# Embedding stage of a two-layer hybrid block: the order of its loads and of VectorE's turns

## Chip, cores and metric

The kernel runs on one core of one Trainium2 chip. The metric is the device time of one execution in microseconds (us), lower is better. The engines are TensorE (PE), VectorE (DVE), ScalarE (ACT), GpSimd (POOL) and SyncE (SP, which here only issues transfers).

## What is computed

A row of 1024 tokens with 1024 features goes through a layer norm and then through two layers, each a projection into a state-space part, latent attention, retention and sparse attention, an output projection, and an MLP:

```python
h = layer_norm(x, ln_emb_g, ln_emb_b)
for l in range(2):
    parts = split_columns(h @ w_in[l])        # the first 260 columns: z (256) and dt (4)
    ...
    h = layer_norm(ALPHA * h + mix, ln1_g[l], ln1_b[l])
    ff = square(relu(h @ w_mlp1[l])) @ w_mlp2[l]
    h = layer_norm(ALPHA * h + ff, ln2_g[l], ln2_b[l])
# layer_norm: (x - mean) * rsqrt(var + 1e-5) * g + b
```

The change touches only the first line and the 260 columns of z and dt of layer 0, which are projected in the same stage.

## The kernel before

The stage `embed` holds the whole of `h` in SBUF as eight tiles of 128 tokens (one token per partition, 1024 features in a row). Products are made to nearly full float32 precision by splitting each operand into a high part (rounded to fp32r) and a low part (the rest), and taking three products: high x high, high x low, low x high. Each engine has its own instruction list; semaphores tie them together, and each engine runs its list in order.

What happens to tile t, and where it stands in the code:
- SP loads `h[:, t, :]` (L195). Behind tile 1 it issues the two loads of z and dt weights (`load_columns`, L338, into `ahead`, seen through `raw`) and the gain row and the bias row of the norm, each spread over all 128 partitions (L198, L199: 512 KB each, as large as a tile).
- VectorE, `moments(t)`: two `bn_stats` (L213), `bn_aggr` (L215), add of epsilon to the variance (L217).
- GpSimd, `rstd(t)`: the power -0.5 of one column (L263).
- VectorE, the shift, -mean x rstd, one column, both inputs in SBUF (L241).
- ScalarE centres the tile: x x rstd + shift (L290).
- VectorE, `finish(t)`: the tile times the gain row, the gain product (L222), both inputs in SBUF.
- GpSimd adds the bias row (L271), both inputs in SBUF. For tile 7 VectorE does it itself (L226). Then the tile is ready (`normed`): SP stores it to `residual` (L204), and TensorE turns it, eight transposes of 128x128 into two banks of PSUM (L323).
- ScalarE, `highs(t)`: two copies from PSUM, the high parts of the turned tile (L285). VectorE, `lows(t)`: two subtractions, PSUM minus high part, the low parts `x_lo` (L233).
- TensorE, `project(t)`: 24 products of the turned tile with the z weights (L363 to L365). ScalarE, `take(t)`: two copies out of PSUM (L278, L279), which also wait until the store of the tile is done, since they overwrite `h`.

Once per stage, the z weights are split: ScalarE copies each half (L295, after it has centred tile 0), VectorE subtracts each half (L246, in turn 0), both inputs in SBUF. Behind that (`w_lo`) SP issues the next weights' load (L203) and then the stores, and TensorE may start its first projection.

The order of VectorE's list is written out by hand: `moments(0)`, and then for each turn t: `moments(t + 1)`, shift(t), in turn 0 the split, `finish(t - 1)`, `lows(t - 3)`. TensorE's: transposes of t, `project(t - 2)`. GpSimd's: `rstd(0)`, `rstd(1)`, and then `rstd(t + 2)`, bias add of t. The stage ends with a barrier of all engines behind the last `take`; the next stage's work begins behind it.

Of the kernel before, what the change touches and what calls it, by code (L numbers as in the profile page):

```python
# [23 lines left out]
ALU = mybir.AluOpType  # L24
# [6 lines left out]
NT = T // P  # L31
# [137 lines left out]
def embed(nc, x, gain, bias, h, dtr, residual, hi, lo, ahead, ident, next_w):  # L169
# [5 lines left out]
    with ExitStack() as c:  # L175
        n = norm_tiles(nc, c, "emb")
# [10 lines left out]
        LAG = 2  # L187
        x_loaded = [s.x_loaded0, s.x_loaded1, s.x_loaded2, s.x_loaded3, s.x_loaded4, s.x_loaded5, s.x_loaded6, s.x_loaded7]
        with nc.Block() as block:
            first_loads = ahead.count + 16 * len(projection_groups()[0].parts)  # L190

            @block.sync
            def _(sp):
                for t in range(NT):
                    sp.dma_start(h[:, t, :], x[t * P:(t + 1) * P, :]).then_inc(x_loaded[t], 16)  # L195
                    if t == 1:
                        load_columns(sp, ahead, next_w, 0)
                        sp.dma_start(n.gain[:], gain.partition_broadcast(P)).then_inc(s.gains_loaded, 16)  # L198
                        sp.dma_start(n.bias[:], bias.partition_broadcast(P)).then_inc(s.gains_loaded, 16)  # L199
                sp.wait_ge(s.w_lo, 2)  # L200
                load_columns(sp, ahead, next_w, 1)
                for t in range(NT):
                    sp.wait_ge(s.normed, t + 1)  # L203
                    sp.dma_start(residual[t * P:(t + 1) * P, :], h[:, t, :]).then_inc(h_stored[t], 16)  # L204
                for t in range(NT):
                    sp.wait_ge(h_stored[t], 16)

            @block.vector
            def _(dve):
                def moments(t):  # L210
                    dve.wait_ge(x_loaded[t], 16)
                    for half in range(2):
                        dve.bn_stats(n.stats[:, t, half, :], h[:, t, half * 512:(half + 1) * 512]).then_inc(s.stats_ready, 1)  # L213
                    dve.wait_ge(s.stats_ready, 2 * t + 2)
                    dve.bn_aggr(n.mv[:, t, :], n.stats[:, t, :, :].rearrange("p a b -> p (a b)")).then_inc(s.moments_ready, 1)  # L215
                    dve.wait_ge(s.moments_ready, t + 1)
                    dve.tensor_scalar(n.var[:, t:t + 1], n.mv[:, t, 1:2], EPS, None, ALU.add).then_inc(s.var_ready, 1)  # L217

                def finish(t):
                    dve.wait_ge(s.centred, t + 1)  # L220
                    dve.wait_ge(s.gains_loaded, 32)
                    dve.tensor_tensor(h[:, t, :], h[:, t, :], n.gain[:], ALU.mult).then_inc(s.scaled, 1)  # L222
                    if t == NT - 1:
                        dve.wait_ge(s.scaled, NT)
                        dve.wait_ge(s.normed, NT - 1)
                        dve.tensor_tensor(h[:, t, :], h[:, t, :], n.bias[:], ALU.add).then_inc(s.normed, 1)  # L226

                def lows(t):
                    for half in range(2):
                        g = 2 * t + half  # L230
                        dve.wait_ge(s.hi_copied, g + 1)
                        part = slice(4 * half, 4 * half + 4)
                        dve.tensor_tensor(lo[:, part, t * P:(t + 1) * P], tr[:, g % 6, :].rearrange("p (k n) -> p k n", k=4),  # L233
                                          hi[:, part, t * P:(t + 1) * P].bitcast(F32), ALU.subtract).then_inc(s.lo_copied, 1)

                moments(0)
                for t in range(NT):
                    if t + 1 < NT:
                        moments(t + 1)
                    dve.wait_ge(s.rstd_ready, t + 1)  # L240
                    dve.scalar_tensor_tensor(n.shift[:, t:t + 1], n.mv[:, t, 0:1], -1.0, n.rstd[:, t:t + 1], ALU.mult,  # L241
                                             ALU.mult).then_inc(s.shift_ready, 1)
                    if t == 0:
                        for part in range(2):
                            dve.wait_ge(s.w_hi, part + 1)
                            dve.tensor_tensor(wlo[:, k_half(part), :], raw[:, k_half(part), :], whi[:, k_half(part), :].bitcast(F32),  # L246
                                              ALU.subtract).then_inc(s.w_lo, 1)
                    if t:
                        finish(t - 1)
                    if t >= 3:  # L250
                        lows(t - 3)
                finish(NT - 1)
                lows(NT - 3)
                lows(NT - 2)
                lows(NT - 1)

            @block.gpsimd
            def _(pool):
                pool.memset(n.power[:], -0.5).then_inc(s.power_set, 1)
                pool.wait_ge(s.power_set, 1)  # L260
                def rstd(t):
                    pool.wait_ge(s.var_ready, t + 1)
                    pool.tensor_tensor(n.rstd[:, t:t + 1], n.var[:, t:t + 1], n.power[:], ALU.pow).then_inc(s.rstd_ready, 1)  # L263

                rstd(0)
                rstd(1)
                for t in range(NT - 1):
                    if t + 2 < NT:
                        rstd(t + 2)
                    pool.wait_ge(s.scaled, t + 1)  # L270
                    pool.tensor_tensor(h[:, t, :], h[:, t, :], n.bias[:], ALU.add).then_inc(s.normed, 1)  # L271

            @block.scalar
            def _(act):
                def take(t):
                    act.wait_ge(s.z_ready, t + 1)
                    act.wait_ge(h_stored[t], 16)
                    act.activation(h[:, t, GW:2 * GW], zp[:, t % 2, 0:GW], ACT.Copy)  # L278
                    act.activation(dtr[:, t, :], zp[:, t % 2, GW:FIRST], ACT.Copy).then_inc(s.z_taken, 1)  # L279

                def highs(t):
                    for half in range(2):
                        g = 2 * t + half
                        act.wait_ge(s.turned, g + 1)
                        act.activation(hi[:, 4 * half:4 * half + 4, t * P:(t + 1) * P], tr[:, g % 6, :].rearrange("p (k n) -> p k n", k=4),  # L285
                                       ACT.Copy).then_inc(s.hi_copied, 1)

                for t in range(NT):
                    act.wait_ge(s.shift_ready, t + 1)
                    act.activation(h[:, t, :], h[:, t, :], ACT.Identity, bias=n.shift[:, t:t + 1],  # L290
                                   scale=n.rstd[:, t:t + 1]).then_inc(s.centred, 1)
                    if t == 0:
                        act.wait_ge(ahead.sem, first_loads)
                        for part in range(2):
                            act.activation(whi[:, k_half(part), :], raw[:, k_half(part), :], ACT.Copy).then_inc(s.w_hi, 1)  # L295
                    if t >= 3:
                        highs(t - 3)
                    if t >= 3 + LAG:
                        take(t - 3 - LAG)
                for t in range(NT - 3, NT):  # L300
                    highs(t)
                    take(t - LAG)
                for t in range(NT - LAG, NT):
                    take(t)

            @block.tensor
            def _(pe):
                def project(t):
                    pe.wait_ge(s.w_lo, 2)
                    pe.wait_ge(s.lo_copied, 2 * t + 2)  # L310
                    if t >= 2:
                        pe.wait_ge(s.z_taken, t - 1)
                    first_unit(pe, zp[:, t % 2, 0:FIRST], hi, lo, whi, wlo, t).then_inc(s.z_ready, 1)

                for t in range(NT):
                    pe.wait_ge(s.normed, t + 1)
                    for half in range(2):
                        g = 2 * t + half
                        if g >= 6:
                            pe.wait_ge(s.lo_copied, g - 5)  # L320
                        for j in range(4):
                            k = 4 * half + j
                            mm = pe.transpose(tr[:, g % 6, j * P:(j + 1) * P], h[:, t, k * P:(k + 1) * P], ident[:])  # L323
                        mm.then_inc(s.turned, 1)
                    if t >= LAG:
                        project(t - LAG)
                for t in range(NT - LAG, NT):
                    project(t)
# [2641 lines left out]
```

## Time and profile before

| | |
|---|---|
| median of 3 runs | 2829.88 us (2828.07 to 2831.41) |
| profiled execution, its own time | 2830.91 us |
| its span in the trace | 2829.1 us |
| mean granted clock of TensorE | 0.977 |
| PE busy | 2658.6 us, 94% |
| DVE busy | 1894.8 us, 67% |
| ACT busy | 1285.5 us, 45% |
| POOL busy | 309.5 us, 11% |
| tile 0 lands / last `take` starts | 7.0 us / 62.97 us |

Times in the trace count from the start of the span. The device time of the profiled execution is 1.8 us more than the span. A granted clock of 1.00 is TensorE at 2.4 GHz, 0.50 is 1.2 GHz. The embedding stage is the first 64 us.

### The profile page before, as it was taken

Reading aid. Unit: us, or ns where it says so; the run is one execution under the profiler, and the core shown is the slowest. Engines: PE = TensorE matmul, PEld = TensorE weight load, DVE = VectorE, ACT = ScalarE, POOL = GpSimd, SP = SyncE. Lnnn points to the kernel's source line nnn. Section 1 sums busy time; section 2 is a strip of 40 time slices with the busy share of each in tenths; the row PEclk is TensorE's granted clock in tenths of the full one; section 3 lists DMA queues with packets and bytes.
Section 4 is the critical chain, followed back from the end, with each engine's and each line's share of the span. In section 5 each row is a group of like instructions: output and inputs, shape, how many; then the busy total and the mean of one; then the engine's idle time right before and its main releaser. Section 6 shows DMA issues by size and latency. Waiting matters only on the chain. (4 is left out here: it accounts for less than half of the span.)

```text
span 2829.1 us, 39315 instructions
## 1 busy us (share of the span) xinstructions
PE 2658.6 (94%) x14644; PEld 2273.5 (80%) x14644; DVE 1894.8 (67%) x2993; ACT 1285.5 (45%) x2327; POOL 309.5 (11%) x304
## 2 busy tenths in 40 slices
PE   5999989888989999999999999898899899999997
PEld 5899868777868887888888998686778688878886
DVE  5654546576777776686856444566766877758778
ACT  3332236666355554433433222556643555543343
POOL 3121223111000000000011212221110000000000
PEclk9999999999999999999999999899999999999998
DMA  4223323102315445987621233330032354479865
GB/s 165 71 68 89 96 80 95 38 1 83 112 62 173 144 143 185 384 316 246 237 86 39 78 100 97 93 90 1 1 125 84 97 164 152 142 266 361 291 228 188
DMA packets 256563, 387.11 MB, mean 137 GB/s; under 512 B 40760, under 2 KB 129272, under 8 KB 256376
## 3 DMA queue, kind: packets, MB, share of 16 engines
q1 hardware_dynamic: 256376, 384.61, 42.1%
q8 instruction: 119, 1.95, 0.3%
q14 instruction: 68, 0.56, 0.1%
HBM read 287.73 MB, written 96.83 MB: 136 GB/s over the span
## 5 line engine op out<-in xcount | busy, mean ns | idle before, releaser
L2863 DVE TENSOR_TENSOR att_el<-att_ET,att_eh 128x512 fp32r<-128x512 f32 (+1 forms) x228 | 151.3, 671 | 97.5 <-ACT att_eh L2805 96.0
L636 POOL TENSOR_TENSOR norm_rstd<-norm_var,norm_power 128x1 f32<-128x1 f32 x32 | 28.9, 904 | 1471.9 <-DVE norm_var L616 1471.9
L1618 PE MATMUL mix_acc<-mix_whi,x_hi 128*128 128x256 f32 (+1 forms) x640 | 185.4, 290 | 0.0
L2805 ACT ACTIVATE att_eh<-att_ET 128x512 fp32r<-128x512 f32 (+1 forms) x228 | 131.6, 584 | 108.7 <-PE att_ET L2713 74.0
L990 PE MATMUL dense_tr<-mlp_w,mlp_a 128*128 128x512 f32 x448 | 175.3, 391 | 5.4 <-DVE mlp_w L1294 5.4
L1620 PE MATMUL mix_acc<-mix_whi,x_lo 128*128 128x256 f32 (+1 forms) x640 | 180.0, 281 | 0.0
L1619 PE MATMUL mix_acc<-mix_wlo,x_hi 128*128 128x256 f32 (+1 forms) x640 | 179.9, 281 | 0.0
L2796 ACT ACTIVATE att_E<-att_S,att_negm 128x64 f32<-128x64 f32 (+8 forms) x256 | 155.4, 616 | 45.6 <-DVE att_negm L2856 29.9
L990 PE MATMUL dense_acc<-mlp_w,mlp_a 128*128 128x512 f32 x448 | 174.8, 390 | 0.0
L992 PE MATMUL dense_tr<-mlp_w,mlp_a 128*128 128x512 f32 x448 | 174.8, 390 | 0.0
L991 PE MATMUL dense_acc<-mlp_w,mlp_a 128*128 128x512 f32 x448 | 174.6, 390 | 0.0
L991 PE MATMUL dense_tr<-mlp_w,mlp_a 128*128 128x512 f32 x448 | 174.6, 390 | 0.0
L992 PE MATMUL dense_acc<-mlp_w,mlp_a 128*128 128x512 f32 x448 | 174.5, 390 | 0.0
L2856 DVE TENSOR_REDUCE att_negm<-att_S 128x1 f32<-128x640 f32 (+12 forms) x160 | 136.6, 860 | 53.4 <-PE att_S L2692 50.0
L1098 ACT ACTIVATE mlp_a<-mlp_a_raw 128x1024 fp32r<-128x1024 f32 x72 | 76.3, 1060 | 166.9 <-PE dense_tr L992 137.7
L2713 PE MATMUL att_ET<-ident,att_E 128*128 128x128 f32 (+1 forms) x880 | 135.3, 279 | 14.0 <-DVE att_el L2863 13.9
L1292 DVE TENSOR_TENSOR mlp_a<-mlp_a_raw,mlp_a 128x1024 fp32r<-128x1024 f32 x72 | 88.0, 1222 | 65.7 <-ACT mlp_a L1098 65.7
L1619 PEld LDWEIGHTS mix_acc<-mix_wlo,x_hi 128*128 128x128 f32 x640 | 122.8, 192 | 0.1
L1618 PEld LDWEIGHTS mix_acc<-mix_whi,x_hi 128*128 128x128 f32 x640 | 122.7, 192 | 0.1
L1583 POOL TENSOR_TENSOR mix_wlo<-ahead,mix_whi 128x2048 fp32r<-128x2048 f32 (+2 forms) x22 | 94.3, 4288 | 258.9 <-ACT mix_whi L1800 258.9
L1620 PEld LDWEIGHTS mix_acc<-mix_whi,x_lo 128*128 128x128 f32 x640 | 122.6, 192 | 0.0
L1233 DVE TENSOR_TENSOR h<-h 128x512 f32<-128x512 f32 x160 | 99.1, 685 | 34.7 <-issue 30.6
(431 smaller groups left out, 7815.4 us busy)
## 6 DMA issues: line engine op xcount, KB each, us to landing
mlp_w_raw<-w_mlp SPq DMA_DIRECT2D x124, 512.0 KB, 6.1
blocks<-h SPq DMA_DIRECT2D x32, 1792.0 KB, 8.8
mlp_a_raw<-blocks SPq DMA_DIRECT2D x72, 512.0 KB, 4.5
mlp_raw<-w_mlp SPq DMA_DIRECT2D x66, 512.0 KB, 6.0
ahead<-w_in SPq DMA_DIRECT2D x20, 1024.0 KB, 6.9
mlp_temp<-blocks SPq DMA_DIRECT2D x38, 512.0 KB, 5.0
residual<-h SPq DMA_DIRECT2D x32, 512.0 KB, 3.2
h<-residual SPq DMA_DIRECT2D x32, 512.0 KB, 6.9
```

What stands on the lines that cost most here:

```text
L990: pe.matmul(out, ah, wh, start=(ch == 0 and k == 0), stop=False, skip_group_check=True)
L991: pe.matmul(out, ah, wl, start=False, stop=False, skip_group_check=True)
L992: mm = pe.matmul(out, al, wh, start=False, stop=(ch == CH - 1 and k == 1), skip_group_check=True)
L1233: mm = dve.tensor_tensor(stage[g % 2][:, i - 1, :], part[a], part[b], op)
L1618: pe.matmul(out, xh, whi[b][:, k, 0:n], start=(k == 0), stop=False)
L1619: pe.matmul(out, xh, wlo[b][:, k, 0:n], start=False, stop=False)
L1620: mm = pe.matmul(out, xl, whi[b][:, k, 0:n], start=False, stop=(k == KT - 1))
L2713: mm = pe.transpose(ET[0:kw, o % 2, j * P:(j + 1) * P], E[:, p.unit % KEPT, at:at + kw], ident[:])
L2796: e = act.activation(E[:, n % KEPT, here], S[:, n % 2, here], ACT.Exp, bias=negm[:, n, r:r + 1], accum_out=den[:, d, h:h + 1])
L2805: act.activation(eh[0:kw, k % RING, cols], ET[0:kw, nth[x] % 2, cols], ACT.Copy).then_inc(s.high_ready, 1)
L2856: dve.tensor_reduce(negm[:, n, first:len(q.rows):step], view[:, first:len(q.rows):step, 0:width], AX.X, ALU.max, negate=True).then_inc(s.m ...
L2863: dve.tensor_tensor(el[0:kw, k % RING, cols], ET[0:kw, nth[x] % 2, cols], eh[0:kw, k % RING, cols].bitcast(F32), ALU.subtract).then_inc(s. ...
```

## The change

The gain and bias rows are issued behind tile 0, the two z loads behind tile 2. In VectorE's list the shift of tile t stands ahead of `moments(t + 1)`; the gain product of tile t comes in turn t instead of turn t + 1; the split of the z weights stands in turn 2 behind that product; `lows(t - 2)` takes the place of `lows(t - 3)`. GpSimd does the bias add of t ahead of `rstd(t + 2)`. ScalarE casts the z weights in turn 2, and its `highs` and `take` come one turn sooner. TensorE's list stays.

```diff
--- before.py
+++ after.py
@@ -193,10 +193,11 @@
             def _(sp):
                 for t in range(NT):
                     sp.dma_start(h[:, t, :], x[t * P:(t + 1) * P, :]).then_inc(x_loaded[t], 16)
-                    if t == 1:
-                        load_columns(sp, ahead, next_w, 0)
+                    if t == 0:
                         sp.dma_start(n.gain[:], gain.partition_broadcast(P)).then_inc(s.gains_loaded, 16)
                         sp.dma_start(n.bias[:], bias.partition_broadcast(P)).then_inc(s.gains_loaded, 16)
+                    if t == 2:
+                        load_columns(sp, ahead, next_w, 0)
                 sp.wait_ge(s.w_lo, 2)
                 load_columns(sp, ahead, next_w, 1)
                 for t in range(NT):
@@ -235,22 +236,19 @@
 
                 moments(0)
                 for t in range(NT):
-                    if t + 1 < NT:
-                        moments(t + 1)
                     dve.wait_ge(s.rstd_ready, t + 1)
                     dve.scalar_tensor_tensor(n.shift[:, t:t + 1], n.mv[:, t, 0:1], -1.0, n.rstd[:, t:t + 1], ALU.mult,
                                              ALU.mult).then_inc(s.shift_ready, 1)
-                    if t == 0:
+                    if t + 1 < NT:
+                        moments(t + 1)
+                    finish(t)
+                    if t == 2:
                         for part in range(2):
                             dve.wait_ge(s.w_hi, part + 1)
                             dve.tensor_tensor(wlo[:, k_half(part), :], raw[:, k_half(part), :], whi[:, k_half(part), :].bitcast(F32),
                                               ALU.subtract).then_inc(s.w_lo, 1)
-                    if t:
-                        finish(t - 1)
-                    if t >= 3:
-                        lows(t - 3)
-                finish(NT - 1)
-                lows(NT - 3)
+                    if t >= 2:
+                        lows(t - 2)
                 lows(NT - 2)
                 lows(NT - 1)
 
@@ -265,10 +263,10 @@
                 rstd(0)
                 rstd(1)
                 for t in range(NT - 1):
+                    pool.wait_ge(s.scaled, t + 1)
+                    pool.tensor_tensor(h[:, t, :], h[:, t, :], n.bias[:], ALU.add).then_inc(s.normed, 1)
                     if t + 2 < NT:
                         rstd(t + 2)
-                    pool.wait_ge(s.scaled, t + 1)
-                    pool.tensor_tensor(h[:, t, :], h[:, t, :], n.bias[:], ALU.add).then_inc(s.normed, 1)
 
             @block.scalar
             def _(act):
@@ -289,15 +287,15 @@
                     act.wait_ge(s.shift_ready, t + 1)
                     act.activation(h[:, t, :], h[:, t, :], ACT.Identity, bias=n.shift[:, t:t + 1],
                                    scale=n.rstd[:, t:t + 1]).then_inc(s.centred, 1)
-                    if t == 0:
+                    if t == 2:
                         act.wait_ge(ahead.sem, first_loads)
                         for part in range(2):
                             act.activation(whi[:, k_half(part), :], raw[:, k_half(part), :], ACT.Copy).then_inc(s.w_hi, 1)
-                    if t >= 3:
-                        highs(t - 3)
-                    if t >= 3 + LAG:
-                        take(t - 3 - LAG)
-                for t in range(NT - 3, NT):
+                    if t >= 2:
+                        highs(t - 2)
+                    if t >= 2 + LAG:
+                        take(t - 2 - LAG)
+                for t in range(NT - 2, NT):
                     highs(t)
                     take(t - LAG)
                 for t in range(NT - LAG, NT):
```

## Rows read from the trace of the kernel before

**Rows 1.** Timeline of ScalarE, embedding
```profile
12.27 2.03 ACT L295 ACTIVATE emb_whi<-ahead 128x1040 fp32r<-128x1040 f32 x2 [0.54 <-DMA ahead<-w_in]
...
23.60 1.24 ACT L290 ACTIVATE h<-h,emb_shift,emb_rstd 128x1024 f32<-128x1024 f32 x1 [2.62 <-DVE emb_shift L241]
...
57.23 0.38 ACT L278 ACTIVATE h<-emb_zp 128x256 f32<-128x256 f32 x1 [2.24 <-PE emb_zp L365]
...
62.97 0.39 ACT L278 ACTIVATE h<-emb_zp 128x256 f32<-128x256 f32 x1 [2.42 <-PE emb_zp L365]
```

**Rows 2.** Timeline of VectorE, embedding: start us, us, what, count [idle before <-releaser]
```profile
13.37 2.40 DVE L246 TENSOR_TENSOR emb_wlo<-ahead,emb_whi 128x1040 fp32r<-128x1040 f32 x2 [2.92 <-ACT emb_whi L295]
...
19.61 1.22 DVE L222 TENSOR_TENSOR h<-h,emb_gain 128x1024 f32<-128x1024 f32 x1
...
22.37 1.19 DVE L241 SCALAR_TENSOR_TENSOR emb_shift<-emb_mv,emb_rstd 128x1 f32<-128x1 f32 x1
...
29.22 1.29 DVE L233 TENSOR_TENSOR x_lo<-emb_tr,x_hi 128x512 fp32r<-128x512 f32 x2 [0.66 <-ACT x_hi L285]
...
32.12 1.22 DVE L222 TENSOR_TENSOR h<-h,emb_gain 128x1024 f32<-128x1024 f32 x1
...
36.89 1.22 DVE L222 TENSOR_TENSOR h<-h,emb_gain 128x1024 f32<-128x1024 f32 x1
...
50.40 1.22 DVE L226 TENSOR_TENSOR h<-h,emb_bias 128x1024 f32<-128x1024 f32 x1
```

**Rows 3.** Timeline of VectorE and GpSimd in the last layer norm
```profile
2807.38 1.29 DVE L609 BATCH_NORM_STATS2 norm_stats<-h 128x6 f32<-128x512 f32 x2
...
2809.03 1.23 DVE L627 TENSOR_TENSOR h<-h,norm_gain 128x1024 f32<-128x1024 f32 x1
...
2809.18 1.48 POOL L636 TENSOR_TENSOR norm_rstd<-norm_var,norm_power 128x1 f32<-128x1 f32 x1 [2.67 <-DVE norm_var L616]
...
2810.70 0.16 DVE L621 SCALAR_TENSOR_TENSOR norm_shift<-norm_mv,norm_rstd 128x1 f32<-128x1 f32 x1 [0.44 <-POOL norm_rstd L636]
```

**Rows 4.** Timeline of GpSimd, embedding
```profile
19.71 1.53 POOL L263 TENSOR_TENSOR emb_rstd<-emb_var,emb_power 128x1 f32<-128x1 f32 x1 [8.68 <-DVE emb_var L217]
21.21 2.33 POOL L271 TENSOR_TENSOR h<-h,emb_bias 128x1024 f32<-128x1024 f32 x1
```

**Rows 5.** Timeline of SP's queue, embedding
```profile
3.42 0.81 SPq L195 DMA_DIRECT2D h<-x  x2
...
8.91 0.43 SPq L199 DMA_DIRECT2D emb_bias<-ln_emb_b  x1
```

**Rows 6.** Landing times of tiles 0 and 1 (L195), then of the bias row (L199)
```profile
DMA to landing us min/median/max: 3.6/4.1/4.5
...
DMA to landing us min/median/max: 7.7/7.7/7.7
```

**Rows 7.** Timeline of GpSimd and VectorE in attention, 1944.9 to 1945.2 us
```profile
1944.93 0.73 POOL L2600 TENSOR_TENSOR h<-h,att_total 128x256 f32<-128x256 f32 x1
1944.96 0.72 DVE L2878 TENSOR_TENSOR att_factor<-att_factor,att_gates 128x4 f32<-128x4 f32 x1
```

**Rows 8.** Timeline of GpSimd and VectorE in the dense part, about 1351 us
```profile
1350.77 1.52 POOL L636 TENSOR_TENSOR norm_rstd<-norm_var,norm_power 128x1 f32<-128x1 f32 x1 [11.10 <-DVE norm_var L616]
...
1351.80 1.22 DVE L1294 TENSOR_TENSOR mlp_w<-mlp_raw,mlp_w 128x1024 fp32r<-128x1024 f32 x1
```

**Rows 9.** Timeline of TensorE: the last eight transposes of the embedding
```profile
53.27 1.03 PE L323 MATMUL emb_tr<-ident,h 128*128 128x128 f32 x8
```

**Rows 10.** Windows: stretch, us, busy (count) by engine, granted clock, DMA share, GB/s
```profile
66.00:70.00 4.00, 4.00 (x12) 3.11 (x11) 1.44 (x3) 0.48 (x1) 0.00 (x0) 0.57 0.49 4
...
383.90:387.30 3.40, 2.10 (x6) 1.25 (x7) 0.00 (x0) 0.00 (x0) 0.00 (x0) 1.00 0.67 216
...
524.00:527.20 3.20, 1.46 (x7) 0.66 (x6) 0.69 (x1) 1.66 (x4) 0.00 (x0) 1.00 0.00 0
527.20:530.60 3.40, 1.12 (x4) 0.72 (x4) 2.49 (x6) 1.29 (x3) 0.62 (x1) 0.50 0.00 0
```

## The prediction

> **What bounds the kernel now.** I read the page first: TensorE is busy for 94% of the span (the table above), so a stage in front of it hands its delay on almost whole. The change touches only the embedding stage, from 3.4 us to the barrier behind the last copy of the projected columns. So I read the timelines of the engines there, one by one, and asked what paces a tile. What ends the stage is TensorE: the copies that wait for a finished projection start at 57.23 and (two tiles later) at 62.97 us, 2.87 us apart, back to back [rows 1]. The reader is to see that TensorE gets there only because VectorE and GpSimd fed it early enough: gain products start some 3.9 us apart at first (19.61, and the second right behind the shift of 22.37) and 4.77 us apart from the fourth on (32.12, 36.89) [rows 2]. A late VectorE would therefore show at the end.
>
> Two facts about that pair of engines carry the argument. First, the shift (0.16 us where nothing is in its way [rows 3]) took 1.19 us at 22.37 and ended at 23.56; GpSimd's bias add ran from 21.21 for 2.33, to 23.54 [rows 2, 4]. A VectorE instruction whose two inputs are in SBUF stands still while GpSimd's add runs; the subtractions of x_lo, with one input in PSUM, took 1.29 for two at 29.22, beside the next add, and lost nothing [rows 2]. Second, the square root behind a gain product ends 0.41 us after the product: 2809.03 + 1.23 = 2810.26 and 2809.18 + 1.48 = 2810.66 [rows 3].
>
> **The change part by part.** *Loads.* SP issues the gain and bias rows behind tile 0. Before, tiles 0 and 1 land at 3.4 + 3.6 = 7.0 and 3.8 + 4.5 = 8.3 us, the bias row at 8.91 + 7.7 = 16.6 [rows 5, 6], and the cast that waits for the z loads starts at 12.27 [rows 1]. Tile 1 now comes behind two more transfers of its own size. Lower bound: each takes the 1.3 us between tiles 0 and 1, so it lands at 7.0 + 3 x 1.3 = 10.9. Upper bound: the two rows take what they took before, 16.6 - 12.3 = 4.3, so 8.3 + 4.3 = 12.6. The rows do not say which holds (whatever drew out the two rows may or may not return), so I take the middle, 11.8. Tile 2 follows 1.3 later and z behind it; both are there before they are asked for. The three SP instructions that change places cost nothing else.
>
> *The moments moved behind the shift.* This is what costs. Before, moments(t+1) ran while GpSimd added the bias of t-1, and then shift and gain product followed at once. Now the order is shift(t), moments(t+1), gain product(t), subtractions(t-2) from tile 2 on, shift(t+1). Counting from the start of gain product(t):
> - the product ends at 1.23; the square root of t+1, asked for just after the product began, ends at 1.23 + 0.41 = 1.64 [rows 3];
> - GpSimd goes straight on to the bias add of t. At 21.21 such an add began 0.03 before the square root ahead of it ended (19.71 + 1.53 = 21.24) [rows 4]; VectorE, waiting for the same square root, begins its shift 0.04 after it (2810.66 to 2810.70) [rows 3]. So the add leads by 0.06 to 0.07 us. In attention a lead of 0.03 us was enough: the add at 1944.93 ran 0.73, the product at 1944.96 took 0.72 for four elements [rows 7]. The shift waits for the whole add, until 1.61 + 2.33 + 0.02 = 3.96. From tile 2 on it comes behind the two subtractions, in the middle of the add, and waits with no doubt;
> - then the moments: from the first statistics to the gain product 2809.03 - 2807.38 = 1.65, and a VectorE instruction behind the shift starts some 0.08 before it ends (2810.70 + 0.16 against 2810.77) [rows 3]. Next product: 3.96 - 0.08 + 1.65 = 5.53.
>
> ScalarE's centring (1.24) [rows 1] lies beside the moments. The subtractions (1.29) lie beside the add. So a turn takes 5.53 us where it took 3.9 or 4.77. The moments were hidden by the add, and the new order takes that cover away; that the bias add comes before the next square root on GpSimd removes nothing, since the add must wait for the product anyway.
>
> *The split of z, two turns later.* In turn 2 ScalarE casts the halves behind its centring (2.03 for both) [rows 1] and VectorE subtracts them, 2.40 for both before [rows 2]. Both inputs are in SBUF. The first half starts right behind the gain product; the small square root that waits then does not delay it (1351.80 took 1.22 with one waiting since 1350.77) [rows 8]. It ends about 2.4 after the product's start. The bias add of tile 2 has waited and now runs to about 2.35 + 2.3 = 4.65; the second half waits for it and ends 1.1 later, 5.75; the subtractions of tile 0 end at 6.95; shift and moments follow (1.65), product 3 starts at about 8.6. A turn of 8.6 instead of 5.53: 3.05 more. Before, the split lay in the wait for tile 2 and cost nothing.
>
> The Trainium skill (SBUF — State Buffer, section Who interferes with whom) says that the SBUF port pair which VectorE and GpSimd share is an exclusive lock, held for the whole instruction. By that sentence the square root would also hold up the first half of the split by 0.4 us, and the sum would be 4.7 where it is 4.3; the row of the trace shows no such delay, and it decides.
>
> *Sum.* With tile 1 at L = 11.8, product 0 starts at L + 1.65 = 13.45. Products 1 and 2: +5.53 each, 24.5. Product 3: +8.6, 33.1. Products 4 to 6: 3 x 5.53, 49.7. Product 7 needs no moments before it, only the centring: 3.96 + 0.04 + 1.24 + 0.03 = 5.27, so 55.0. The bias add of tile 7 on VectorE ends 2.5 later (1.23 + 0.03 + 1.22 [rows 2]), 57.5; subtractions of tile 5, 1.2, end at 58.7. TensorE by then has turned tile 7 (1.0 [rows 9]) and has three projections left: 3 x 2.87 + 0.03 = 8.65 [rows 1]. Last copy at about 67.3 instead of 62.97: **+4.3 us**. With the bounds for L, 66.4 to 68.1: +3.4 to +5.1. TensorE's own work (1.0 + 2.9 a turn) fits in 5.53 and is no bound from tile 3 on. The stores of the rows queue behind the later w_lo wait on SP, and behind them ScalarE's copies wait, but these come a turn of 5 us later still; I cost that at nothing. If a store were late there, it would hold the centring behind the copy and cost what it is late.
>
> The profiled execution took 2830.91 for a span of 2829.1, 1.0 above the median of 2829.88. Its sum gives 2835.2; against the median I predict **2834.2 us**. A measurement of this kernel tells about 0.2% (5.7 us) from no change, so this is a loss inside that bound.
>
> **The rivals.**
> 1. *My forecast*, the shift held up in every turn: +3.4 to +5.1, chance 0.62. The stage's end also meets TensorE's clock: behind it came 4.0 us with a mean granted clock of 0.57 [rows 10], which is 3.4 us at 1.2 instead of 2.4 GHz and loses 1.7 of work. Whether that returns at the shifted time moves the result by up to that.
> 2. *The shift slips in ahead of the add* in turns 0 and 1, since only 0.06 us decide. Then the moments lie beside the add, the next product starts at its end, 3.95, and two turns save 1.58 each: +4.3 - 3.2 = +1.1, 2831.0. The row with a lead of 0.03 speaks against it. Chance 0.11.
> 3. *The clock falls inside the stage* (the one that ends slower by over 0.2%). TensorE is busy for 3.9 of 5.53 us from tile 3 on. In a stretch with 2.10 of 3.40 us busy it kept 1.00; behind one with 1.46 of 3.20 it ran at 0.50 [rows 10]. My share, 0.71, is above both, but it is made of idle gaps of 1.6 us. One such fall in the last turns costs about 1.7 (three projections that nothing hides), 2834.2 + 1.7 = 2835.9; two give 2837.6. It decides only if it falls from product 6 on; earlier the idle 1.6 us a turn take it up. Chance 0.19.
> 4. *VectorE is not held up as I think*, for instance because the 1.19 us of the old shift have another cause. Then a turn is VectorE's own 1.15 + 1.2 + 0.07 + 1.65 = 4.1, the early rows pay, and TensorE becomes the bound: first projection at about 28, eight projections of 2.87 and five turnings of 1.0 end at 56.0, and half of the first at the lower clock adds 1.4: 57.4, -5.5, 2824.4. Against it stand the matching ends of shift and add. Chance 0.08.
>
> **How the numbers follow.** The likeliest is rival 1's middle, 2834.2; its own range is 2833.3 to 2835.0 by L alone, 2831.6 to 2836.7 with the clock. The 8-in-10 range takes in rival 2 and most of rival 3: 2830.0 to 2837.5. Slower by over 0.2% (above 2835.5): rival 3 with 0.13 of its 0.19, and 0.13 from the upper end of rival 1: 0.26. Faster (below 2824.2): half of rival 4, 0.04. Within: 0.70.
>
> **What would show it.** In the profile after: gain products 5.5 us apart with a gap of 8.6 behind the third; all shifts but the first at over 2 us (turns 0 and 1) or some 1.5 (later), ending with a bias add; the second half of the split at over 2 us; tile 1's statistics at 10.9 to 12.6; the last copy of emb_zp at 66.4 to 68.1. Shifts of 0.15 in turns 1 and 2 mean rival 2, in all turns rival 4. A granted clock below 1.00 between 45 and 68 us means rival 3. Wrong outright would be a stage end before 63 us, or one past 70, which would mean a wait for a store or a load that I cost at nothing.

## The result, and the profile after

The changed kernel has a median of 2835.12 us (22 runs, 2829.66 to 2837.51) against 2829.30 us of 22 runs of the kernel before beside it: ratio 1.0019 [1.0013, 1.0025]. It is slower by 5.8 us, a loss that the measurement tells from zero. It lies on the edge of the prediction's bound of 0.2%: the ratio is just inside (0.19%), the two medians just outside (5.8 for 5.7 us). It is 0.9 above the predicted 2834.2, and inside its range. The last copy of emb_zp, which closes the embedding stage, starts at 68.11 us instead of 62.97: +5.14, just at the upper end of the +3.4 to +5.1 that the prediction gave. The profiled span is 2833.7 us with a mean granted clock of 0.978.

Busy times of the engines, from the page of the changed kernel:

```profile
PE 2658.4 (94%) x14644; PEld 2272.2 (80%) x14644; DVE 1903.8 (67%) x2993; ACT 1284.7 (45%) x2327; POOL 310.0 (11%) x304
```

TensorE does what it did. VectorE is "busy" for 9.0 us more with the same instructions, 8.9 of it in the embedding (39.3 us of the first 64 before, 48.2 of the first 69 now): a VectorE instruction that stands still behind GpSimd is counted as running, so the waits hide in durations and not in idle time. Timeline of VectorE in the embedding (start us, us, what, count, idle before it and its releaser), which answers to [rows 2]:

```profile
12.40 1.29 DVE L214 BATCH_NORM_STATS2 emb_stats<-h 128x6 f32<-128x512 f32 x2 [3.04 <-DMA h<-x]
...
14.05 1.23 DVE L223 TENSOR_TENSOR h<-h,emb_gain 128x1024 f32<-128x1024 f32 x1
15.73 2.29 DVE L240 SCALAR_TENSOR_TENSOR emb_shift<-emb_mv,emb_rstd 128x1 f32<-128x1 f32 x1 [0.45 <-POOL emb_rstd L261]
...
19.57 1.23 DVE L223 TENSOR_TENSOR h<-h,emb_gain 128x1024 f32<-128x1024 f32 x1
...
25.07 1.23 DVE L223 TENSOR_TENSOR h<-h,emb_gain 128x1024 f32<-128x1024 f32 x1
26.22 4.53 DVE L248 TENSOR_TENSOR emb_wlo<-ahead,emb_whi 128x1040 fp32r<-128x1040 f32 x2
...
33.57 1.22 DVE L223 TENSOR_TENSOR h<-h,emb_gain 128x1024 f32<-128x1024 f32 x1
34.71 1.28 DVE L234 TENSOR_TENSOR x_lo<-emb_tr,x_hi 128x512 fp32r<-128x512 f32 x2
35.91 1.63 DVE L240 SCALAR_TENSOR_TENSOR emb_shift<-emb_mv,emb_rstd 128x1 f32<-128x1 f32 x1
...
39.10 1.23 DVE L223 TENSOR_TENSOR h<-h,emb_gain 128x1024 f32<-128x1024 f32 x1
...
55.43 1.22 DVE L223 TENSOR_TENSOR h<-h,emb_gain 128x1024 f32<-128x1024 f32 x1 [1.31 <-ACT h L288]
56.69 1.23 DVE L227 TENSOR_TENSOR h<-h,emb_bias 128x1024 f32<-128x1024 f32 x1
```

Timeline of GpSimd in the same stretch, which answers to [rows 4]:

```profile
15.66 2.33 POOL L267 TENSOR_TENSOR h<-h,emb_bias 128x1024 f32<-128x1024 f32 x1
...
25.23 1.48 POOL L261 TENSOR_TENSOR emb_rstd<-emb_var,emb_power 128x1 f32<-128x1 f32 x1 [1.72 <-DVE emb_var L218]
26.68 2.97 POOL L267 TENSOR_TENSOR h<-h,emb_bias 128x1024 f32<-128x1024 f32 x1
...
35.17 2.35 POOL L267 TENSOR_TENSOR h<-h,emb_bias 128x1024 f32<-128x1024 f32 x1
```

Read the two side by side. The shift at 15.73 writes one column, and takes 2.29 us: it ends at 18.02, the add of 15.66 at 17.99. The add had a lead of 0.07 us. The shift at 35.91 comes in the middle of the add of 35.17 and ends at 37.54, the add at 37.52. Gain products start 5.52, 5.50, 8.50, and then 5.53 us apart; the last gap is 5.28.

Timeline of ScalarE, the last copies that wait for a projection, against those of [rows 1]; then the eight transposes of tile 7 on TensorE; then the window from 45 to 68 us (busy time and count of PE, PEld, DVE, ACT and POOL, granted clock, DMA share, GB/s):

```profile
65.24 0.38 ACT L276 ACTIVATE h<-emb_zp 128x256 f32<-128x256 f32 x1 [2.43 <-PE emb_zp L363]
...
68.11 0.38 ACT L276 ACTIVATE h<-emb_zp 128x256 f32<-128x256 f32 x1 [2.42 <-PE emb_zp L363]
```

```profile
57.99 1.08 PE L321 MATMUL emb_tr<-ident,h 128*128 128x128 f32 x8
```

```profile
45.00:68.00 23.00, 19.76 (x162) 18.99 (x160) 15.10 (x20) 9.15 (x23) 7.38 (x4) 1.00 0.18 74
```

Behind VectorE's last add (56.69 + 1.23 = 57.92) come one turning on TensorE, beside the subtractions of tile 5 on VectorE, and three projections, at the full clock.

### The profile page after: what moved, and what is told of

It is laid out like the page before. It is cut to its first block and busy times, and to the rows that moved or that the text cites. A ratio compares the mean times of both kernels' runs of the same rounds, so it can differ in the third digit from the quotient of the medians.

```text
span 2833.7 us, 39315 instructions
## 1 busy us (share of the span) xinstructions
PE 2658.4 (94%) x14644; PEld 2272.2 (80%) x14644; DVE 1903.8 (67%) x2993; ACT 1284.7 (45%) x2327; POOL 310.0 (11%) x304
```

## The experiments

Every kernel below has 10 or 11 runs, timed against 33 runs of the kernel before on the same chip (medians 2829.29 and 2829.24 on the two chips used); the change itself has 22 against 22. "Stage end" is the start of the last copy of emb_zp in one profiled execution. It is the cleaner measure, but not to the last tenths: in the five kernels with the rows behind tile 0 (the change among them), tile 1 landed between 11.87 and 12.40 us. Whole spans carry TensorE's clock in the other 2760 us with them (a span of 2819.9 with 0.981 and one of 2833.7 with 0.978 lie 13.8 apart, and their stage ends 8.5).

| kernel | stage end | median, us | ratio to before |
|---|---|---|---|
| before | 62.97 | 2829.3 | |
| the change | 68.11 | 2835.12 | 1.0019 [1.0013, 1.0025] |
| change, one-input shift | 59.65 | 2826.01 | 0.9989 [0.9980, 0.9998] |
| before, one-input shift | 62.22 | 2829.57 | 0.9998 [0.9990, 1.0007] |
| change, moments ahead | 68.91 | 2835.39 | 1.0022 [1.0013, 1.0031] |
| loads and split alone | 63.59 | 2830.09 | 1.0000 [0.9992, 1.0009] |
| order alone | 65.13 | 2831.47 | 1.0011 [1.0002, 1.0020] |
| change, rows behind tile 1 | 63.67 | 2830.52 | 1.0005 [0.9996, 1.0014] |
| change, low parts between halves | 66.54 | 2833.02 | 1.0014 [1.0005, 1.0023] |
| order alone, one-input shift | 56.63 | 2824.11 | 0.9982 [0.9973, 0.9991] |

### The shift with one input

The theory is that the shift is held because both its inputs are tiles in SBUF. So the same product is written with the rstd as the scalar operand and only the mean as input, in the changed kernel, where it should free the loop, and in the kernel before, where the add paces the loop anyway.

```diff
-dve.scalar_tensor_tensor(n.shift[:, t:t + 1], n.mv[:, t, 0:1], -1.0, n.rstd[:, t:t + 1], ALU.mult,
-                         ALU.mult).then_inc(s.shift_ready, 1)
+dve.tensor_scalar(n.shift[:, t:t + 1], n.mv[:, t, 0:1], n.rstd[:, t:t + 1], -1.0, ALU.mult,
+                  ALU.mult).then_inc(s.shift_ready, 1)
```

> The changed kernel, with the shift computed from one SBUF tensor and a per-partition scalar (tensor_scalar) in place of two SBUF tensors (scalar_tensor_tensor); same numbers. My theory: the shift no longer waits for GpSimd's bias add. Shifts take about 0.15 us in every turn, gain products come 4.0 to 4.1 us apart where the changed kernel has 5.53, TensorE becomes the bound behind tile 6 and the last copy of emb_zp starts at 60 to 61 us (68.1 in the changed kernel, 62.97 before): 7 to 8 us faster than the changed kernel, some 2 us faster than before. Rival A, the wait belongs to GpSimd's add whatever form the shift has: nothing moves, last copy at 68.1, shifts of 1.6 to 2.3 us. Rival B, the shift's wait is only a symptom and moments, centring or loads set the turn: shifts of 0.15 us but turns still above 5 us.

> The kernel before, with the same one-input shift. My theory: there the shift's wait was hidden, because the gain product behind it has to wait for the end of the same bias add. Last copy of emb_zp within 0.3 us of 62.97, ratio to before 1.000. The rival, that the wait had cost the kernel before as well, gives the last copy up to 2 us earlier (two waits of 1.0 us at 22.4 and 26.2 us).

Timeline of all engines in the changed kernel with this shift, 15.0 to 17.6 us:

```profile
15.23 2.34 POOL L267 TENSOR_TENSOR h<-h,emb_bias 128x1024 f32<-128x1024 f32 x1
15.29 0.21 DVE L240 TENSOR_SCALAR emb_shift<-emb_mv,emb_rstd 128x1 f32<-128x1 f32 x1 [0.45 <-POOL emb_rstd L261]
15.42 1.27 DVE L214 BATCH_NORM_STATS2 emb_stats<-h 128x6 f32<-128x512 f32 x2
...
17.05 1.60 DVE L223 TENSOR_TENSOR h<-h,emb_gain 128x1024 f32<-128x1024 f32 x1
```

Same place, same lead of the add (0.06 us), and the shift takes 0.21 us where it took 2.29. The moments now lie beside the add, and the product itself, which has two inputs, waits for its end (17.57) and takes 1.60. From tile 3 on the turn is 4.09 us, where it was 5.53. The stage ends 8.46 us sooner than with the change (0.43 of it tile 1, that landed sooner, at 11.97) and 3.32 sooner than before. So the hold on this one instruction is what the change pays for, and without it the rest of the change would have been a gain: 2826.01, 0.9989 [0.9980, 0.9998].

The Trainium skill (SBUF — State Buffer, section Who interferes with whom) says that a VectorE instruction with at most one SBUF input, outside the two-port modes, does not contend with GpSimd, and that one with two does where GpSimd reads SBUF. The trace agrees: 0.21 us against 2.29 beside the same add. The edit changes the instruction too, and not only its inputs; but the gain product, another instruction with two inputs in SBUF, is held in this kernel and the next (1.60 and 2.13), and the subtractions, with one input in PSUM, are not (1.29 in the next kernel, at 33.13, beside the add of 32.85).

In the kernel before, all engines from 21 to 24 us:

```profile
21.18 2.33 POOL L271 TENSOR_TENSOR h<-h,emb_bias 128x1024 f32<-128x1024 f32 x1
...
22.34 0.20 DVE L241 TENSOR_SCALAR emb_shift<-emb_mv,emb_rstd 128x1 f32<-128x1 f32 x1
22.46 2.13 DVE L222 TENSOR_TENSOR h<-h,emb_gain 128x1024 f32<-128x1024 f32 x1
```

The shift is free here too, and most of the wait moves into the product behind it: 22.46 + 2.13 = 24.59, where before the shift was 22.37 + 1.19 and the product then took 1.21, to 24.69. The stage ends at 62.22, 0.75 sooner, where 62.97 within 0.3 was expected: a small miss, since a shift that is held also holds up ScalarE. ScalarE's and VectorE's timelines in this kernel, tile 0:

```profile
27.52 1.06 ACT L285 ACTIVATE x_hi<-emb_tr 128x512 fp32r<-128x512 f32 x2
28.32 1.27 DVE L233 TENSOR_TENSOR x_lo<-emb_tr,x_hi 128x512 fp32r<-128x512 f32 x2
```

In ScalarE's list the centring of tile 3 stands ahead of these copies. In the kernel before, the shift of tile 3, held to 27.43, let the centring start at 27.47 and the copies at 28.61, and VectorE stood idle 0.66 us for them before the subtractions of 29.22 [rows 2]. Here the centring starts at 26.38, and the subtractions follow the product at once, 0.90 sooner. The fourth gain product starts at 31.25 instead of 32.12, and VectorE's last add at 49.57 instead of 50.40 [rows 2]: the lead is won once and kept. The whole time does not show it (0.9998 [0.9990, 1.0007]).

### The moments ahead of the shift again

The prediction named the place of the moments as what costs. Here they go back ahead of the shift, and all else of the change stays.

```diff
                 for t in range(NT):
+                    if t + 1 < NT:
+                        moments(t + 1)
                     dve.wait_ge(s.rstd_ready, t + 1)
                     dve.scalar_tensor_tensor(n.shift[:, t:t + 1], n.mv[:, t, 0:1], -1.0, n.rstd[:, t:t + 1], ALU.mult,
                                              ALU.mult).then_inc(s.shift_ready, 1)
-                    if t + 1 < NT:
-                        moments(t + 1)
                     finish(t)
```

> The changed kernel with moments(t + 1) put back ahead of the shift of t; the product stays in the same turn as its shift. My prediction named the moments behind the shift as what costs. If that place alone is the cause, turns fall from 5.53 to about 4.1 us and the last copy comes at about 60 us. My present reckoning is another: the moments then lie beside the add, but the product of t now waits for shift and centring of t behind them (0.15 + 1.24 + hand-overs), so a turn is 1.15 + 1.2 + 1.6 + 1.45 = 5.4 us with subtractions and 4.9 without, product 0 comes 1.4 later, and the last copy is at 68 to 69 us, no earlier than in the changed kernel (68.1).

The stage ends at 68.91, no sooner than with the change. Timeline of VectorE in this kernel, tiles 1 and 3:

```profile
17.93 0.89 DVE L242 SCALAR_TENSOR_TENSOR emb_shift<-emb_mv,emb_rstd 128x1 f32<-128x1 f32 x1
20.13 1.22 DVE L223 TENSOR_TENSOR h<-h,emb_gain 128x1024 f32<-128x1024 f32 x1 [1.31 <-ACT h L288]
...
33.51 0.15 DVE L242 SCALAR_TENSOR_TENSOR emb_shift<-emb_mv,emb_rstd 128x1 f32<-128x1 f32 x1
34.97 1.23 DVE L223 TENSOR_TENSOR h<-h,emb_gain 128x1024 f32<-128x1024 f32 x1 [1.31 <-ACT h L288]
```

The shift is held less (0.89) or not at all (0.15 for tiles 3 to 6), and yet the turns are 4.97, 4.96, 9.88, and then 5.43, 5.42, 5.42: the product stands right behind its own shift, with nothing between, and waits 1.31 us for ScalarE's centring. So the place of the moments alone is not the cause. By these rows, what costs is that a tile's shift, centring and product are now in one turn of VectorE, one behind the other; no run moves the product alone. The changed kernel fills ScalarE's 1.24 us with the moments and pays for the held shift; this one lays the moments beside the add and pays for ScalarE. The two cost nearly the same.

In this kernel the granted clock did fall inside the stage. The window from 38 to 42 us, in the order of [rows 10]:

```profile
38.00:42.00 4.00, 3.32 (x16) 3.33 (x17) 2.62 (x6) 2.54 (x5) 1.47 (x3) 0.60 0.73 299
```

TensorE had been idle for 2.01 us before the transposes of tile 3 began at 38.68, and they take 1.93 us instead of 1.10. A granted clock of 0.60 is a mix of the two levels, 2.4 and 1.2 GHz. It cost the end nothing: from the last gain product to the last copy it is 12.68 us here (56.23 to 68.91) and in the changed kernel (55.43 to 68.11). That is what the prediction's rival 3 says of a fall ahead of product 6.

### Loads and split alone, order alone

The first keeps the order of the kernel before and moves only the loads, the split and its casts, as below; the second is every other line of the change's diff.

```diff
-                    if t == 1:
-                        load_columns(sp, ahead, next_w, 0)
+                    if t == 0:
                         sp.dma_start(n.gain[:], gain.partition_broadcast(P)).then_inc(s.gains_loaded, 16)
                         sp.dma_start(n.bias[:], bias.partition_broadcast(P)).then_inc(s.gains_loaded, 16)
+                    if t == 2:
+                        load_columns(sp, ahead, next_w, 0)
...
-                    if t == 0:
+                    if t == 2:
                         for part in range(2):
                             dve.wait_ge(s.w_hi, part + 1)
...
-                    if t == 0:
+                    if t == 2:
                         act.wait_ge(ahead.sem, first_loads)
```

> The kernel before with only the loads and the split of the z weights moved (rows behind tile 0, z behind tile 2, split and casts in turn 2); VectorE's order, GpSimd's and the lows, highs and takes stay. Expected: product 0 at 15.5 us instead of 19.61, but the split stands ahead of product 1 and waits for the casts behind the centring, so product 1 comes at 24.9 instead of 23.48; last copy 63.7 to 64.4, that is 0.7 to 1.4 us slower than before. The rival, that the early rows pay in full, gives a last copy 2 to 4 us earlier than 62.97.

> The changed kernel with the loads and the split of z put back (rows and z behind tile 1, casts and split in turn 0, between moments of tile 1 and product 0): the new order of shift, moments, product and subtractions alone. My theory: product 0 at 16.7 us (the bias row lands at 16.6), product 1 at about 20.3, then 5.53 us a turn with no long turn: last copy at about 65.5, 2.5 us slower than before, 2.6 faster than the changed kernel (the long turn of 8.5 is gone, 3.0, and the late rows cost 2.6 less the cheap first turn). If the order costs nothing and the loads and the split do, the last copy is at 63.

Loads and split alone: the split waits for ScalarE's casts (VectorE's timeline), and the stage ends at 63.59, 0.1 under the expected 63.7 to 64.4:

```profile
22.09 2.39 DVE L247 TENSOR_TENSOR emb_wlo<-ahead,emb_whi 128x1040 fp32r<-128x1040 f32 x2 [2.27 <-ACT emb_whi L296]
```

Order alone: 65.13, 0.4 under the 65.5 expected. All engines, 17.0 to 21.3 us:

```profile
17.16 0.15 DVE L239 SCALAR_TENSOR_TENSOR emb_shift<-emb_mv,emb_rstd 128x1 f32<-128x1 f32 x1
...
17.32 2.35 POOL L266 TENSOR_TENSOR h<-h,emb_bias 128x1024 f32<-128x1024 f32 x1 [5.41 <-DVE h L222]
...
18.92 1.83 DVE L222 TENSOR_TENSOR h<-h,emb_gain 128x1024 f32<-128x1024 f32 x1
...
21.13 2.33 POOL L266 TENSOR_TENSOR h<-h,emb_bias 128x1024 f32<-128x1024 f32 x1
21.19 2.29 DVE L239 SCALAR_TENSOR_TENSOR emb_shift<-emb_mv,emb_rstd 128x1 f32<-128x1 f32 x1 [0.44 <-POOL emb_rstd L260]
```

This one timeline shows both outcomes of the race between shift and add. Tile 1 and its square root are there early, so the shift at 17.16 follows the product at once, 0.16 us ahead of the add, and takes 0.15; the next turn is 2.90 us. At 21.19 the shift had to wait for the square root, the add is 0.06 ahead, and it takes 2.29. That is the prediction's rival 2 in turn 0 and its forecast in turn 1.

In the first, the rival that the early rows pay in full fell: product 0 comes at 15.26 instead of 19.61, and the split takes that back, product 1 at 24.40 instead of 23.48.

The parts cost 0.62 and 2.16, together 2.78; the change costs 5.14. From order alone to the change, up to the fourth product (30.55 to 33.57, 3.02): product 0 starts 1.97 sooner (14.05 for 16.02), the first gap is 2.62 longer (the slip is lost, since tile 1 is late behind the two rows), the second 0.62 shorter, and the third 2.99 longer (the split in it). The late tile and the split are cheap in the old order and dear in the new one.

### The rows behind tile 1

If the late tile 1 is what loses the slip, then the rows one place later restore it.

```diff
                     sp.dma_start(h[:, t, :], x[t * P:(t + 1) * P, :]).then_inc(x_loaded[t], 16)
-                    if t == 0:
+                    if t == 1:
                         sp.dma_start(n.gain[:], gain.partition_broadcast(P)).then_inc(s.gains_loaded, 16)
```

> The changed kernel with the gain and bias rows issued behind tile 1 instead of tile 0 (z stays behind tile 2). Theory: the late landing of tile 1 (12.4 us) holds up moments(1), product 0 and with it every later turn. Here tile 1 lands at 8 us, the square root of tile 1 is long done, and product 0 starts when the rows land, at about 12.4 us instead of 14.05; shift 1 starts ahead of the bias add of tile 0 and takes 0.15 us, so that product 2 starts about 9 us behind product 0 instead of 11.0. From then on nothing changes. Last copy at 64 to 65 us (68.1 in the changed kernel), still later than before (62.97). If the landing of tile 1 doesn't matter, it stays at 68.

All engines, 11.5 to 13.0 us:

```profile
11.59 1.23 DVE L223 TENSOR_TENSOR h<-h,emb_gain 128x1024 f32<-128x1024 f32 x1 [0.37 <-DMA emb_bias<-ln_emb_b]
12.73 0.15 DVE L240 SCALAR_TENSOR_TENSOR emb_shift<-emb_mv,emb_rstd 128x1 f32<-128x1 f32 x1
12.89 2.35 POOL L267 TENSOR_TENSOR h<-h,emb_bias 128x1024 f32<-128x1024 f32 x1 [1.04 <-DVE h L223]
```

It does: the shift slips in 0.16 us ahead, the first gap is 2.97 instead of 5.52, product 0 comes 2.46 sooner, and the stage ends at 63.67, a little under the expected 64 to 65. The two rows moved by one place are worth 4.4 us of stage, of which 2.5 is the product's earlier start and 2.0 what is left of the slip once the second gap grows (6.05 for 5.50).

### The low parts between the halves of the split

The prediction says that the second half of the split waits for the bias add of tile 2. The subtractions of tile 0, with one input in PSUM, could use that time.

```diff
                     if t == 2:
                         for part in range(2):
+                            if part == 1:
+                                lows(0)
                             dve.wait_ge(s.w_hi, part + 1)
...
-                    if t >= 2:
+                    if t >= 3:
                         lows(t - 2)
```

> The changed kernel with the two subtractions lows(0) between the two halves of the z split in turn 2. Theory: the second half waits 2.2 us for the bias add because both want the shared port; subtractions with one input in PSUM can run in that time. The long turn falls from 8.5 to 7.3 us, the second half takes about 2.1 us in place of 3.38, and the last copy comes 1.2 us earlier, at 66.9. If the length of the long turn were only the sum of VectorE's work in order, the swap would change nothing: 68.1.

First the changed kernel (VectorE, the second half of the split, a narrow window), then this one (all engines, 25.7 to 30.4 us):

```profile
27.37 3.38 DVE L248 TENSOR_TENSOR emb_wlo<-ahead,emb_whi 128x1040 fp32r<-128x1040 f32 x1
```

```profile
26.27 2.98 POOL L269 TENSOR_TENSOR h<-h,emb_bias 128x1024 f32<-128x1024 f32 x1
26.96 1.28 DVE L234 TENSOR_TENSOR x_lo<-emb_tr,x_hi 128x512 fp32r<-128x512 f32 x2
28.16 2.18 DVE L250 TENSOR_TENSOR emb_wlo<-ahead,emb_whi 128x1040 fp32r<-128x1040 f32 x1
```

The half takes 2.18 instead of 3.38 and ends 1.1 behind the add either way (29.65 there, 29.25 here); the subtractions run beside the add for nothing. The long turn is 7.30 instead of 8.50, and the stage ends at 66.54: 1.57 sooner, of which 0.41 is tile 1, that landed sooner here (11.99), and 1.2 the edit.

### Order alone with the one-input shift

The loads and the split stay where they were before, the order is the new one, and the shift has one input. The edit is the one of the first experiment, in order alone.

> The new order with the loads and the split where they were before the change, and the one-input shift: the version the runs so far point to. Product 0 at 16.0, turns of 2.9 and 3.8 at first, 4.1 from product 2 on, no long turn: product 7 at about 43.2, last copy at 56.5 to 57.5 us, 5.5 to 6.5 us earlier than before: ratio to before 0.9979. Rival: TensorE becomes the bound (8 projections of 2.87 and 5 turnings of 1.03 behind the first subtraction, and the lower clock at first) and the gain stops at 58 to 59 us.

All engines, 24 to 27 us, then ScalarE's last copy:

```profile
24.26 2.34 POOL L266 TENSOR_TENSOR h<-h,emb_bias 128x1024 f32<-128x1024 f32 x1
25.01 0.20 DVE L239 TENSOR_SCALAR emb_shift<-emb_mv,emb_rstd 128x1 f32<-128x1 f32 x1
...
26.75 1.23 DVE L222 TENSOR_TENSOR h<-h,emb_gain 128x1024 f32<-128x1024 f32 x1
```

```profile
56.63 0.38 ACT L275 ACTIVATE h<-emb_zp 128x256 f32<-128x256 f32 x1 [2.42 <-PE emb_zp L362]
```

Turns of 4.1 us from tile 3 on, the stage 6.34 us sooner than before, and 2824.11 us, 0.9982 [0.9973, 0.9991]: it beats both kernels. It is not VectorE that ends this stage. The window from 32 to 56 us:

```profile
32.00:56.00 24.00, 24.00 (x205) 23.92 (x204) 15.58 (x28) 11.58 (x27) 10.56 (x6) 1.00 0.26 103
```

By the profile TensorE is busy without a gap, at the full clock, so behind 32 us a still faster VectorE would give nothing more. The rival named the right bound, but its time was too late: 58 to 59 for 56.63.

## Why the prediction was right

**The held shift** was right to the hundredth: 2.29 us behind an add with a lead of 0.07 (it said 0.06 to 0.07), 1.63 from tile 4 on, where it comes behind two subtractions, turns of 5.50 to 5.53 for 5.53. That the two inputs are the reason is shown by the one-input shift. One of the signs was off: it says all shifts but the first, but the shift of tile 3 (31.87) took 0.14, since the split had outlasted the add. The sum has it right, with 1.65 for shift and moments there.

**The naming of the cause** was too narrow. "The moments moved behind the shift. This is what costs" does not hold by itself: with the moments back, the stage ends later still. The step that is right is the sum of the turn, held shift plus moments; what the prediction left out is that the turn has a second bound of nearly the same length, held or waiting on ScalarE, as long as product and shift of a tile share it.

**The long turn** was 8.50 for 8.6. Its parts are there: the first half undelayed, the second at 3.38, ending 1.1 behind the add. In the changed kernel, all engines about 26.5 us:

```profile
26.22 1.23 DVE L248 TENSOR_TENSOR emb_wlo<-ahead,emb_whi 128x1040 fp32r<-128x1040 f32 x1
```

The square root of 25.23 was still waiting when the half began, ended at 26.71 in the middle of it, and did not hold it up. The Trainium skill (SBUF — State Buffer, section Who interferes with whom) calls the pair an exclusive lock, with the other side fully blocked for the whole instruction. By that sentence and these rows, an estimate, the half would have taken some 0.4 more. The row shows 1.23, the same as an undisturbed one, and decides.

**Tile 1** was the term that was mis-sized: it landed at 12.40 where 11.8 was taken, inside the bounds of 10.9 and 12.6. The four other kernels with the rows behind tile 0 have 11.87 to 12.06, so up to half a microsecond of it belongs to this one execution. SP issues the bias row at 4.20. From the trace of the changed kernel, the view of that line (L198):

```profile
DMA to landing us min/median/max: 6.9/6.9/6.9
```

It lands at 11.1, 2.8 behind the gain row (3.72 + 4.6 = 8.3), and tile 1 comes 1.3 behind that. The drawing out of the two rows that the upper bound rested on (4.3 for both) came with them to the new place: 1.6 + 2.8 = 4.4.

**The sum.** Of the 0.81 us between 67.3 and 68.11, 0.60 is tile 1. The last gap was 5.28, and products 0 to 7 together took 0.17 less than the sum has. The tail was 0.38 more. Up to the subtractions of tile 5 it is right: they end 3.7 us behind the start of product 7, forecast (55.0 to 58.7) and measured (55.43 to 59.12), with the transposes of tile 7 beside them (57.99 to 59.07). What was left out lies behind: the first projection starts at 59.22, 0.10 later, and its copy at 62.36, 3.14 behind it, where the sum has 2.87 + 0.03. The 2.87 is the distance between two copies of projections back to back, and the first of a row takes longer.

**The rivals.** Rival 2 did not happen, and the experiments show its mechanism: a shift 0.16 us ahead is free, one 0.06 behind is held whole, and between the two nothing was measured. It needs a square root that is already there. In both kernels where it happened that was so in turn 0 alone, and the next shift was held for 2.29. So its price of 3.2 us for two turns was too high: there the first two gaps together were 9.02 us instead of 11.02, 2.0 less. Rival 3 did not happen: the clock was 1.00 from 45 to 68 us. The fall behind the stage, which rival 1 leaves open, came again and moved with it. From 71 to 75 us in the changed kernel, against 66 to 70 in [rows 10]:

```profile
71.00:75.00 4.00, 4.00 (x11) 3.13 (x12) 1.61 (x3) 0.65 (x2) 0.00 (x0) 0.57 0.52 4
```

Rival 4 fell with the first shift. Its turn of 4.1 is the 4.09 of the one-input shift, and its first projection at about 28 the 28.25 of that kernel, but the stage ends at 59.65 where it said 57.4. It had TensorE busy from there on. TensorE's timeline in the changed kernel with the one-input shift:

```profile
33.81 1.10 PE L321 MATMUL emb_tr<-ident,h 128*128 128x128 f32 x8 [1.36 <-POOL h L267]
```

TensorE stands idle 1.36 us for the bias add of tile 3, whose product comes late behind the split (a turn of 8.92, its second half still waiting for the add). The other 0.9 of the difference was not followed up.

**The bound of 0.2%.** 0.19% slower, with an interval of 0.13% to 0.25%, lies on the edge between the two cases to which the prediction gave 0.70 and 0.26, and on which side it fell is luck. The stage accounts for 5.1 of the 5.8 us. The other 0.7 needs no cause: the interval is 3.7 to 7.1 us, and in the two profiled executions the spans lie 4.6 apart with stage ends 5.1 apart.

## What to carry to other kernels

When two engines hold each other up, count the inputs of the smallest instruction that stands between them: one column with two SBUF inputs took 2.3 us in the first turns and 1.6 later, the same column with one input 0.2, and the turns went from 5.5 to 4.1 us. Before an order is changed, write down for each turn what lies beside the long instruction of the other engine. Two edits that each cost little may take away each other's cover (0.6 and 2.2 apart, 5.1 together), so time them apart and together.

## What the runs showed that was not expected

- A hold inside an instruction is counted as busy: VectorE's 9.0 us more come with the same 2993 instructions, and idle time shows nothing of them.
- The small square root on GpSimd is held too: it takes 1.48 beside a gain product and ends some 0.4 us behind it, and 0.55 where nothing is in its way (at 18.76 in the kernel with the moments ahead). Yet the split's first half, right behind such a product, went on undelayed (1.23).
- The hold goes both ways: the bias add of 26.68, begun while the first half of the split ran (to 27.45), took 2.97 instead of 2.33.
- Of two rows of the same 512 KB, issued one behind the other, the gain row landed 1.6 us behind tile 0 and the bias row 2.8 behind the gain row, while a tile of the same size took 1.3.
